# Sample attention in the last phase of a streaming-encoder step: value products from split float32 parts, new keys as a third block, the mask moved into the scan

## What is computed

```
def _sb_block(q, qpos, k, v, kpos):
    z = jnp.einsum('bqhd,bkhd->bhqk', q, k) * HEAD_DIM ** -0.5
    causal = kpos[None, :] < qpos[:, None]
    log_keep = jnp.where(causal, jax.nn.log_sigmoid(-z), 0.0)
    rev = lax.cumsum(log_keep, axis=log_keep.ndim - 1, reverse=True)
    after = jnp.concatenate([rev[..., 1:], jnp.zeros_like(rev[..., :1])], axis=-1)
    log_a = jnp.where(causal, jax.nn.log_sigmoid(z) + after, -jnp.inf)
    a = jnp.exp(log_a)
    return jnp.einsum('bhqk,bkhd->bqhd', a, v)
...
k_all = jnp.concatenate([past_k, k_new], axis=1)      # 256 + 16 keys
v_all = jnp.concatenate([past_v, v_new], axis=1)
...
h = (jax.nn.silu(z) * o) @ b_w_out
x = x + _rmsnorm(h, b_norm_post)
```

## Time and profile before

| | |
|---|---|
| median of 3 executions | 2989.13 us (2986.16 to 2991.53) |
| the profiled execution | 2988.19 us, span 2986.6 us |
| PE busy over the span | 96% |
| DVE, ACT, POOL busy | 54%, 44%, 39% |
| mean granted TensorE clock | 0.988 |
| last phase | 2684.4 us to the end, about 302 us |
| PE busy in its steady part | 34.00 of 34 us in each of five stretches |
| POOL busy there | 2.7 of 34 us |
| DVE busy there | 19.5 of 34 us |

### The profile page before, as it was taken

One profiled execution on the slowest core, in us unless ns is written; L12 is line 12 of the kernel. 1 busy time (PEld: TensorE's weight loads), 2 busy tenths in 40 slices (PEclk: granted clock), 3 DMA queues, 4 the chain that ended last, 5 costly groups with the idle time before them and its releaser, 6 DMA issues. The chain is left out here.

```text
span 2986.6 us, 41974 instructions
## 1 busy us (share of the span) xinstructions
PE 2855.2 (96%) x14824; PEld 2457.8 (82%) x14824; DVE 1624.5 (54%) x2112; ACT 1324.5 (44%) x2738; POOL 1153.0 (39%) x1013
## 2 busy tenths in 40 slices
PE   7999999999899899999999999999999999989998
PEld 6999999999788788899788888888888877867776
DVE  5322123221343521022388888888888899886554
ACT  6000010000233511111377777777777788774332
POOL 3333233332120110012366666666667576651000
PEclk9999999999999999999999999999999999999999
DMA  5111111110254345344786767676767677856763
GB/s 157 32 33 29 36 36 36 27 37 29 101 148 140 106 158 179 121 142 154 214 233 188 226 184 224 186 226 183 234 179 230 184 233 219 270 183 208 222 208 104
DMA packets 286307, 451.09 MB, mean 151 GB/s; under 512 B 52899, under 2 KB 223011, under 8 KB 280133
## 3 DMA queue, kind: packets, MB, share of 16 engines
q1 hardware_dynamic: 275108, 409.23, 45.0%
q0 software_dynamic: 11040, 39.86, 4.5%
HBM read 325.22 MB, written 123.81 MB: 150 GB/s over the span
## 5 line engine op out<-in xcount | busy, mean ns | idle before, releaser
L1578 POOL TENSOR_TENSOR a_a<-a_a,a_prod 128x512 f32<-128x512 f32 (+3 forms) x640 | 664.1, 1048 | 423.3 <-DVE a_prod L1529 284.9
L1529 DVE TENSOR_TENSOR_SCAN a_prod<-a_keep,a_prod,a_restart 128x513 f32<-128x513 f32 x384 | 488.2, 1272 | 0.2 <-ACT a_keep L1471 0.2
L1537 DVE TENSOR_TENSOR a_atl<-a_pt,a_ath 128x512 fp32r<-128x512 f32 (+3 forms) x640 | 379.7, 597 | 122.9 <-ACT a_ath L1478 119.6
L1470 ACT ACTIVATE a_a<-a_pz 128x512 f32<-128x512 f32 (+3 forms) x640 | 352.5, 551 | 173.8 <-PE a_pz L1393 154.2
L1478 ACT ACTIVATE a_ath<-a_pt 128x512 fp32r<-128x512 f32 (+3 forms) x640 | 349.4, 556 | 93.1 <-PE a_pt L1418 91.3
L1471 ACT ACTIVATE a_keep<-a_pz 128x512 f32<-128x512 f32 (+3 forms) x640 | 354.1, 553 | 0.0
L1418 PE MATMUL a_pt<-ident,a_a 128*128 128x128 f32 x2176 | 343.9, 273 | 9.9 <-DVE a_atl L1537 6.9
L1418 PEld LDWEIGHTS a_pt<-ident,a_a 128*128 128x128 f32 x2176 | 273.4, 141 | 66.8 <-POOL a_a L1578 13.6
L1403 PE MATMUL a_po<-a_ath,a_v 128*128 128x512 f32 (+3 forms) x640 | 287.3, 449 | 42.4 <-DVE a_atl L1537 21.3
L1392 PE MATMUL a_pz<-a_kh,a_q 128*128 128x512 f32 (+3 forms) x640 | 239.6, 376 | 15.8 <-ACT a_keep L1471 11.2
L274 POOL TENSOR_TENSOR w_wh<-w_raw,w_gain 128x1024 fp32r<-128x1024 f32 x22 | 41.7, 1895 | 530.8 <-PE v_pg L343 274.5
(11 more groups left out here) (209 smaller groups left out, 6013.1 us busy)
## 6 DMA issues: line engine op xcount, KB each, us to landing
a_x<-x_d SPq DMA_DIRECT2D x96, 896.0 KB, 4.7
a_x<-x_d SPq DMA_DIRECT2D x64, 832.0 KB, 5.3
a_kh<-kh_t SPq DMA_DIRECT2D x32, 512.0 KB, 10.7
a_kl<-kl_t SPq DMA_DIRECT2D x32, 512.0 KB, 14.4
w_raw<-in_a_w_in POOLq DMA_DIRECT2D x30, 512.0 KB, 4.8
f_y_in<-y_t SPq DMA_DIRECT2D x17, 512.0 KB, 6.7
x<-f_xn POOLq DMA_DIRECT2D x17, 512.0 KB, 6.0
g_y_in<-sz_t SPq DMA_DIRECT2D x17, 512.0 KB, 6.9
```

Of the source, the lines that this page charges most:

```text
L1470: act.activation(a[:, s, q, 0:w], pz[:, n % ZS, 0:w], ACT.Sigmoid, scale=SCALE)
L1529: dve.tensor_tensor_scan(prod[:, s, 0:w + 1][:, ::-1], keep[:, n % KS, 0:w + 1][:, ::-1], restart[:, 0:1].broadcast_to([P, w + 1]), prod[: ...
L1537: dve.tensor_tensor(atl[:, b % AS, c0:], pt[:, turn_slot(hh, b), c0:], ath[:, b % AS, c0:].bitcast(F32), ALU.subtract).then_inc(at_split, 1)
L1578: pool.tensor_tensor(part, part, prod[:, n % PS, after:after + w], ALU.mult).then_inc(weighted, 1)
```

## The change

The values of a stream are loaded into three blocks of 128 rows (`v_in`, now `[128, 3, 1024]`): two of the cache, and a third that POOL clears with a memset and whose last 16 rows the new values fill. POOL then splits all three into `vh` and `vl` (`split_v`: one cast and one subtraction of 128x3072 each); `vl` lies where `v_in` lay. The weights of the last 128 keys are transposed as the third block; its rows beyond the 16 new ones meet zeros. ACT copies the transposed weights as `ath`, DVE subtracts to `atl` (`low_weighted`, new), and PE makes three matmuls of parts for each block. The mask matmul and its two casts are gone: the scan now adds `restart`, a tile that is 1 at each query's own position and 0 elsewhere, to the running product, which puts 1 there and 0 behind it. `load_v` waits for `v_open` (the memset), which waits for `av_done`. `o_t` takes the place of `qh`; `ath` and `atl` that of `keep` and `prod`, so `weights` waits for `weighted`.

```diff
-        v_in = sb("s_v_in", [P, KB, D])
-        vn_in = sb("s_vn_in", [NQ, D])
...
+        NV = KB + 1
+        v_in, vl = (nc.alloc_sbuf_tensor_at("s_" + n, [P, NV, D], dt, offset=v_at)
+                    for n, dt in (("v_in", F32), ("vl", F32R)))
+        vh = sb("s_vh", [P, NV, D], F32R)
...
             def load_v(b):
+                sp.wait_ge(v_open, b + 1)
+                apart(sp, passed_sp)
                 for kb in range(KB):
                     sp.dma_start(v_in[:, kb, :], cache_v[b, kb * P:(kb + 1) * P, :]).then_inc(v_loaded, 16)
-                sp.dma_start(vn_in[:, :], v_sample[bass.ds(b * NQ, NQ), :]).then_inc(v_loaded, 16)
+                sp.dma_start(v_in[P - NQ:P, KB, :], v_sample[bass.ds(b * NQ, NQ), :]).then_inc(v_loaded, 16)
...
+            def split_v(b):
+                pool.wait_ge(v_loaded, 16 * NV * (b + 1))
+                apart(pool, passed)
+                pool.tensor_copy(vh[:, :, :], v_in[:, :, :]).then_inc(v_hi, 1)
+                pool.wait_ge(v_hi, b + 1)
+                pool.tensor_tensor(vl[:, :, :], v_in[:, :, :], vh[:, :, :].bitcast(F32),
+                                   ALU.subtract).then_inc(v_ready, 1)
...
+                if not is_step(j, NB - 1):
+                    pool.wait_ge(av_done, 2 * j + 2)
+                    apart(pool, passed)
+                    pool.memset(v_in[:, KB, :], 0.0).then_inc(v_open, 1)
                 store(j, 0)
-
+                if not is_step(j, NB - 1):
+                    split_v(j + 1)
+
+            pool.memset(v_in[:, KB, :], 0.0).then_inc(v_open, 1)
...
             pads(0)
+            for s in range(2):
+                pool.wait_ge(o_stored[s], 32 * H * NGQ // 2)
+            apart(pool, passed)
+            pool.memset(restart[:, 0:PAST], 0.0).then_inc(restart_set, 1)
+            pool.tensor_copy(restart[:, PAST:NK], first_s[:, :]).then_inc(restart_set, 1)
+            split_v(0)
...
-                        pe.matmul(o, lo, kh, start=False, stop=False)
-                    pe.matmul(pzo[:, f, PAST:NK], identr[:, :], mask_r[:, :], start=False, stop=True)                        .then_inc(z_ready, 1)
+                        mm = pe.matmul(o, lo, kh, start=False, stop=(i == HP - 1))
+                    mm.then_inc(z_ready, 1)
...
             def weigh(b):
-                pe.wait_ge(v_loaded, 16 * (KB + 1) * (b + 1))
+                pe.wait_ge(v_ready, b + 1)
                 for f in range(2):
-                    pe.wait_ge(at_ready, 4 * b + 2 * (f + 1))
+                    pe.wait_ge(at_ready, 2 * b + f + 1)
                     cols = slice(f * W, (f + 1) * W)
-                    for kb in range(KB):
-                        pe.matmul(pzo[:, f, :], at[f][:, kb, :], v_in[:, kb, cols], start=(kb == 0), stop=False)
-                    pe.matmul(pzo[:, f, :], at[f][0:NQ, KB, :], vn_in[:, cols], start=False, stop=True)                        .then_inc(av_done, 1)
+                    o = pzo[:, f, :]
+                    for kb in range(NV):
+                        pe.matmul(o, ath[f][:, kb, :], vh[:, kb, cols], start=(kb == 0), stop=False)
+                        pe.matmul(o, ath[f][:, kb, :], vl[:, kb, cols], start=False, stop=False)
+                        mm = pe.matmul(o, atl[f][:, kb, :], vh[:, kb, cols], start=False, stop=(kb == NV - 1))
+                    mm.then_inc(av_done, 1)
...
-                    dve.tensor_tensor_scan(prod[:, f, 0:NK][:, ::-1], keep[:, f, :][:, ::-1],
-                                           keep[:, f, :][:, ::-1], 1.0, ALU.mult, ALU.bypass).then_inc(scanned, 1)
+                    dve.tensor_tensor_scan(prod[:, f, :][:, ::-1], keep[:, f, :][:, ::-1],
+                                           restart[:, ::-1], 0.0, ALU.mult, ALU.add).then_inc(scanned, 1)
...
+            def low_weighted(b):
+                for f in range(2):
+                    dve.wait_ge(at_hi, 2 * b + f + 1)
+                    dve.tensor_tensor(atl[f][:, :, :], pka[:, f, 0:NV, :], ath[f][:, :, :].bitcast(F32),
+                                      ALU.subtract).then_inc(at_ready, 1)
```

More of the change, by code:

```diff
@@ L102, in make_tools, with phase_norm_in @@
     return sb, pb, sem, sem2
-def phase_norm_in(nc, x_prompt, x_sample, ident, ident_in, epsb, xh, xl, consts, rounded, order, gain_in, room, pg):
+def phase_norm_in(nc, x_prompt, x_sample, ident, ident_in, epsb, xh, xl, consts, order, gain_in, room, pg):
     with ExitStack() as ctx:
@@ L1677, in feature_major, with phase_finish @@
     return ap.rearrange("(kt p) t -> p kt t", p=P)
-def phase_finish(nc, ahead, at_weights, top, cache_v, v_sample, ident, epsb, identr, mask_r, o_stored, post_gain,
+def phase_finish(nc, ahead, at_weights, top, cache_v, v_sample, ident, epsb, first_s, o_stored, post_gain,
                  out_prompt, out_sample):
@@ L1691, in phase_finish @@
         NROUND = KB * KT // 4
+        KEYS_AT = [kb * P for kb in range(KB)] + [NK - P]
         raw, wl, k_in, y_in, x_io = ahead.raw, ahead.wl, ahead.k_in, ahead.y_in, ahead.x_io
@@ L1702, in phase_finish @@
         pad_h, pad_l = (sb(f"s_{n}", [P, 2, HP * PAD], F32R) for n in ("pad_h", "pad_l"))
-        v_in = sb("s_v_in", [P, KB, D])
-        vn_in = sb("s_vn_in", [NQ, D])
+        NV = KB + 1
+        v_at = (nc.sbuf_base + 31) // 32 * 32
+        sb("s_v_room", [P, NV * D])
+        v_in, vl = (nc.alloc_sbuf_tensor_at("s_" + n, [P, NV, D], dt, offset=v_at)
+                    for n, dt in (("v_in", F32), ("vl", F32R)))
+        vh = sb("s_vh", [P, NV, D], F32R)
         kth, ktl = (sb(f"s_{n}", [P, KT, NK], F32R) for n in ("kth", "ktl"))
         a = sb("s_a", [P, 2, NK])
-        keep = sb("s_keep", [P, 2, NK])
-        prod = sb("s_prod", [P, 2, NK + 1])
-        at = [sb(f"s_at{f}", [P, KB + 1, P]) for f in range(2)]
+        at_at = (nc.sbuf_base + 31) // 32 * 32
+        sb("s_at_room", [P, 4 * NV * P])
+        shared = lambda name, shape, dt, at: nc.alloc_sbuf_tensor_at(name, shape, dt, offset=at_at + at)
+        keep, prod = (shared("s_" + n, [P, 2, NK], F32, i * 2 * NK * 4) for i, n in enumerate(("keep", "prod")))
+        ath, atl = ([shared(f"s_{n}{f}", [P, NV, P], F32R, (2 * i + f) * NV * P * 4) for f in range(2)]
+                    for i, n in enumerate(("ath", "atl")))
+        restart = sb("s_restart", [P, NK])
         own = sb("s_own", [P, 2, P])
-        o_t = sb("s_o_t", [P, KT, P])
+        o_t = qh
         ph = pb("g_ph", [P, 2, D])
@@ L1863, in turn_keys @@
                     if not is_step(b, 0):
-                        pe.wait_ge(at_ready, 4 * b)
+                        pe.wait_ge(at_ready, 2 * b)
                 for r, slot, kb, i0 in rounds(first, end):
@@ L1962, in squash @@
                     act.wait_ge(z_ready, 2 * b + f + 1)
-                    act.activation(a[:, f, :], pzo[:, f, 0:NK], ACT.Sigmoid, scale=SCALE)
+                    act.activation(a[:, f, 0:NK - 1], pzo[:, f, 0:NK - 1], ACT.Sigmoid, scale=SCALE)
                     act.activation(keep[:, f, :], pzo[:, f, 0:NK], ACT.Sigmoid, scale=-SCALE).then_inc(z_used, 1)
             def weights(b):
+                act.wait_ge(weighted, 2 * b + 2)
                 for f in range(2):
                     act.wait_ge(a_turned, 2 * b + f + 1)
-                    act.activation(at[f][:, 0:KB, :], pka[:, f, 0:KB, :], ACT.Copy).then_inc(at_ready, 1)
-                    act.activation(at[f][0:NQ, KB, :], pka[0:NQ, f, KB, :], ACT.Copy).then_inc(at_ready, 1)
+                    act.activation(ath[f][:, :, :], pka[:, f, 0:NV, :], ACT.Copy).then_inc(at_hi, 1)
             def out(b):
@@ L2089, in step @@
                     low(j, 1)
+                low_weighted(j)
                 if not is_step(j, NB - 1):
@@ L2108, in _ @@
             dve.wait_ge(cleared, 3)
+            dve.wait_ge(restart_set, 2)
             scan(0)
@@ L2190, in build @@
                      late, at_top, early, o_stored, ahead)
-        phase_finish(nc, ahead, at_weights, top, cache_v.rearrange("b t h d -> b t (h d)"), vs, ident, epsb, identr, mask_sr,
+        phase_finish(nc, ahead, at_weights, top, cache_v.rearrange("b t h d -> b t (h d)"), vs, ident, epsb, first_s,
                      o_stored, b_norm_post[0], yp, ysm)
@@ L2208 @@
     arrays["ident"] = np.eye(P, dtype=np.float32)
-    arrays["mask_s"] = np.where(np.arange(NQ)[None, :] >= np.arange(P)[:, None] % NQ, MASKED, 0.0)\
+    arrays["first_s"] = np.where(np.arange(NQ)[None, :] == np.arange(P)[:, None] % NQ, 1.0, 0.0)\
         .astype(np.float32)
```

29 lines of the change are left out of this document (12 added, 17 removed).

## The result

| | before | after |
|---|---|---|
| median of 5 executions | 2989.13 us (2986.16 to 2993.95) | 3006.31 us (3001.57 to 3010.45) |
| ratio | 1 | 1.0054, 95% interval 1.0042 to 1.0066 |
| the profiled execution | 2988.19 us, span 2986.6 | 3010.45 us, span 3008.9 |
| first VectorE instruction of the last phase (S) | 2684.46 | 2689.06 |
| S to weigh(0) | 30.6 | 41.1 |

A step is the time from one weigh to the next; W is the start of the weigh that begins it. Within the last phase the change costs 319.8 - 302.1 = 17.7 us, which is the 17.2 between the medians. So I compare by phases from here on.

The account below looks back on a forecast made before the run. PE, busy for 96% of the span, was taken to set each step. Start +12.6, step 0 +10.7, steps 1 to 6 +1.3 and step 7 -1.7 sum to 22.9, so 2988.2 becomes 3011 us; range 2996 to 3046.

Parts of the forecast that it names:

- Start, +12.6: Start of the last phase: POOL's split delays low_weights and PE's first projection matmul, then half clock: 12.6 us lost.
- The hold of 9.8: Start of the last phase: POOL's cast and subtraction hold DVE's two-SBUF-input instructions for 3.0 + 6.8 = 9.8 us.
- The clock's share: Start of the last phase: after 10 us of idling PE restarts at half clock, 2.8 us lost, 0 the other end.
- Step 0, +10.7: Step 0: cast before whole's last instruction, subtraction before low; PE waits 11 us and loses clock: weigh(1) at W + 40.4.
- Steps 1 to 6, +0.2 each: Loop steps: the subtraction holds the scan, eating PE's 1.9 us saved and 0.2 more: 34.1 against 33.88, 1.3 together.
- PE's gain: PE's matmuls in the last phase: 14.9 us given back if nothing else happened, weigh saving 1.69 a step.
- The masks' 1.4: Mask matmuls removed from PE: 0.12 us saved twice a step, 1.4 us in six steps.
- Step 7, -1.7: Last step, where nothing is split: PE's saving stands, 1.7 us less.
- POOL's prices: POOL's new work per stream: memset 0.95 us, cast 3.0, subtraction 6.8; 10.8 us in all.
- the cast ahead of whole's last instruction: Rival for the loop steps: the cast gets in first there too, +3.8 to +6.6 a step, 3033 to 3050; chance 0.22.
- a hold covers only part of a long instruction: Rival: DVE gets in after at most 2.4 us, so PE's saving stands: 2973 to 2980, faster; chance 0.1.
- the second rival: Step 0 goes like the loop, or the clock does not fall: 2998 to 3006 us; chance 0.2.

Follow-up runs that it names:

- PE kept at work: The changed kernel with 84 and 94 idle transposes on PE in its two gaps, at the start and in step 0: 2999.95 us, 1.0049.
- the order run: The changed kernel with one more wait: in each step POOL asks for the split only after whole's last instruction: 2998.86 us, 1.0041.
- the mask alone: The kernel before with only the mask part: no mask matmuls or first-phase casts, the scan adds the restart tile: 2986.76 us, 1.0008.
- late at the start: The changed kernel with only stream 0's split made to wait for all eight low_weights, steps unchanged: 2988.44 us, 1.0006.

## Why the prediction was right, and where it was off

The direction, the range (2996 to 3046) and the cause held; the time was 4.7 us, 0.16%, above the median measured. Its sum against the phases:

- **Start, +12.6:** measured +10.5. The hold of 9.8 was right in kind: PE waited 9.66 us, its first projection matmul came 9.0 later than before (S + 21.4, not 12.4), and moving the split away gave 8.7. The clock's share was mis-sized: 2.8 taken from a stretch of 5.7 us at half clock, but here PE was back after some 3 us, and the run with PE kept at work gives 1.3. I had named 0 as the other end.
- **Step 0, +10.7:** measured +10.8. The cast asked at W + 11.9 (12.5 predicted), before whole's last pair (the sum had it hold the last instruction and the subtraction hold low: one instruction off, the same for PE), PE waited 10.88 us, and the clock cost 2.7. The order decides it, as said: 5.0 us from the one wait in the order run, 7.0 where the cast came 1.3 us later.
- **Steps 1 to 6, +0.2 each:** measured -0.3 to -0.4 each, -2.1 together instead of +1.3. This is the step that failed in sign: the cast asked at W + 13.3, not 13.7, the scan was held until W + 25.1, not 25.7, and PE stood 0.9 us at the two weights; over a step without holds the loss was 33.53 - 32.25 = 1.3, where the sum had 34.1 - 31.95 = 2.15. The mechanism (the scan behind the subtraction, PE behind the weights) is in the rows; its price was 0.9 a step too high, and PE's own step 0.3 too low.
- **PE's gain:** the 18 matmuls of weigh took 4.27 us from the start of the first to what follows, not 4.14. The masks' 1.4 gave nothing, by the run with the mask alone. PE's own step without holds is 32.25, not the 31.95 that I had.
- **Step 7, -1.7:** measured -1.5.
- **POOL's prices:** cast 3.0 taken, 2.75 where nobody stood before it; subtraction 6.8 taken, 6.79 alone (late at the start), 7.65 in the mean with DVE's instruction ahead of it.

Of the rivals, the cast ahead of whole's last instruction stayed in step 0 and never reached the loop: there it asked 0.4 us after that instruction began, so the margin was as thin as I had said. That a hold covers only part of a long instruction fell at once: 7.37 and 7.56 stand in the rows. The measured 3006.3 lies at the upper end of the second rival (2998 to 3006), but not by its mechanism: step 0 went the bad way, and the clock did fall. The errors of the terms did not cancel: the phase lost 17.7 us, not 22.9.

## What to carry to other kernels

Idle time of an engine is not free if what it does holds off an engine that the bottleneck waits for: POOL was idle for more than half of the span, and its 10 us per stream cost 28 us against the same 10 us of writing only. Put such work where the other engine has nothing two-input to do that the bottleneck waits for, give it to ScalarE, or cut it in pieces; two waits of one line each moved the result from 0.5% slower to 0.15 to 0.2% faster (0.9985 and 0.9980). Where two engines exclude each other, look at the order in which they ask: here asking 1.3 us later was worth 7.

## What I had not expected of the hardware

- The turn passes from one to the other: at the start of the phase, with both engines queueing, each got one instruction. POOL's small casts of 64x128, 0.29 us alone, took 1.06 to 1.28 each beside DVE's low_weights, which grew from 4.62 to 5.00 for four.
- The scan with two SBUF operands is held like an addition (0.72 to 7.37); the prediction had assumed it from its operands alone. So is its multiplication (0.44 to 6.80 in the order run).
- After idle times of nearly the same length (9.7 and 10.9 us) PE came back to full clock after some 3 us in one case and 6 in the other. No run here settles why.
